# Three attentions with 16-bit value parts in column halves, odd units split by GpSimd, and norms from a sum of six squares

## The chip, the cores and the metric

The kernel runs on one core of one Trainium2 chip. The metric is device time in microseconds (us) of one execution, from the runs' own clock. A TensorE matmul has a stationary operand (loaded first) and a moving one that streams through; results go to PSUM, eight banks of 512 fp32 columns per partition. VectorE and ScalarE read PSUM; GpSimd works in SBUF alone.

## The reference, cut to what matters

512 tokens of width 1024 pass through two transformer blocks. The first has a sparse attention (8 heads of 64; each query attends to its 128 best keys of an index score, keys and values are shared by the heads), a pooling mixer and a layer of 16,384 small experts; the second has a windowed attention (16 heads on 4 key and value heads, window 128, a sink logit per head) and a latent attention (16 heads, query and key width 96, value width 64). Each block ends its parts with root-mean-square norms:

```python
p = jax.nn.softmax(logits, axis=-1)                       # all three attentions
o = jnp.einsum('...hqk,...khd->...qhd', p, v)             # 64 wide per head
h = h + (o * jax.nn.silu(z)) @ w_out                      # window and latent
y_attn = o @ w_up_attn                                    # sparse
y = x * lax.rsqrt(jnp.mean(x * x, axis=-1) + EPS) * g     # every norm, over 1024 features
```

## The kernel before, in words

Activations lie transposed: features on partitions (eight blocks of 128), 512 tokens in the free dimension. Dense products are made in 16-bit parts: each fp32 operand is split into a high part (the value rounded to 16 bit) and a low part (the rest), and `three` (line 830) issues three 16-bit matmuls, high x high, high x low, low x high. Weight tiles of 128 x 1024 come from memory into a ring of four (`ring`), GpSimd scales and splits them (`cut_tile`, lines 753 to 756) into a second ring of four (`parts`). A tile is cut when the tile three before it has begun to be used (`begun`).

`features_wide` starts a projection with the first five input blocks for four outputs, then finishes output by output; it takes a new weight tile per output, so it needs four tiles early. `tokens` makes rows by token: for a group of columns it first awaits four free banks and then sums into all four. Of each stage the sums are taken from PSUM by ScalarE or by VectorE, as a table at the top says (`taker`); a bank is free when that engine has taken its sum.

An attention is a list of units, one per head and block of 128 queries. For unit u in turn TensorE makes the scores in fp32 (`scores`, line 967, banks 4 and 5), VectorE takes the negated maximum (with mask or slope added in the sparse and window kinds; lines 1636, 1642, 1651), ScalarE the exponentials and their sum (line 1319), TensorE transposes the probabilities in blocks of 128 (`turn_probs`, line 976, banks 6 and 7), ScalarE copies them to SBUF (`copy`, line 1275), and TensorE multiplies them in fp32 with the values (`values`, line 988): the probabilities are stationary, 64 value columns move, and the output has tokens on partitions (bank 0 or 1, eight units to a bank). After eight units VectorE divides by the sums (lines 1668, 1671). The order on each engine is written out by hand: at step u TensorE does scores of u, transposes of u - 1 or u - 2 and values of the unit before that; the others follow by semaphores. In the latent kind each head's query and key rows are transposed first (lines 1237, 1240, banks 2 and 3) and copied by VectorE (line 2148), once per four units. GpSimd has no part in an attention.

When all units are done, the outputs are transposed back on TensorE (`turn`, line 959), VectorE multiplies them with the gate (line 2081, window and latent) and splits them (lines 1616, 1617), block by block, and the projection reads them.

Before the latent attention ScalarE takes queries, keys and values (`b_q`, `b_kv`) from PSUM, while VectorE rotates 32 columns of each query head (`rope`, lines 2124 to 2130).

A norm: ScalarE squares the eight blocks (line 1281), TensorE sums each over the partitions by a matmul with ones (`norm_part`, line 911, all eight summed in one bank), ScalarE takes the root, VectorE the reciprocal (line 1583), and then both make the split normed blocks that the next stage reads. The eight `norm_part` matmuls are placed between the outputs of the stage in front, two or more outputs behind the block that they square (`behind`, `late_pairs`, `last_parts`).

## Time and profile before

| | us |
|---|---|
| median of three runs | 2348.11 (2346.35 to 2356.07) |
| profiled execution, own time | 2350.81 |
| its span, first to last instruction | 2349.0 |
| TensorE busy | 2212.0 |
| VectorE busy | 1505.7 |
| GpSimd busy | 1372.1 |
| ScalarE busy | 909.2 |

The span is what the trace covers; the execution's own time also has what lies around it, 1.8 us. Matmuls are pipelined, so one lasts longer than the distance to the next. Read spacing by the starts. An fp32 matmul appears as two records. Of the span the sparse attention takes 222 to 275 us, the window attention 1704 to 1796, the latent one 2056 to 2212.

### The profile page before, as it was taken

To read this page: it belongs to the slowest core of one execution; us is meant where nothing else is said; L and a number is where in the kernel's file an instruction comes from. 1 tells how busy PE (TensorE), PEld (TensorE's weight loads), DVE (VectorE), ACT (ScalarE), POOL (GpSimd) and SP (SyncE) were. 2 spreads that over 40 slices of the span, in tenths; PEclk is the share of its full clock that TensorE was granted. 3 is DMA by queue.
4 is the path that set the end of the run, shared out by engine and by line. 5 is a ranking of instruction groups with operands and counts; after the bars stand their busy time and mean duration, and the time that the engine had idled before them with its cause. 6 is when DMAs were issued, how large, how long until landed. Compare 5 with 4: busy or idle time off the path is not lost. (4 is left out here: it accounts for less than half of the span.)

```text
span 2349.0 us, 36538 instructions
## 1 busy us (share of the span) xinstructions
PE 2212.0 (94%) x12904; PEld 1255.2 (53%) x12904; DVE 1505.7 (64%) x2703; ACT 909.2 (39%) x1582; POOL 1372.1 (58%) x872
## 2 busy tenths in 40 slices
PE   5998988999989999989999999998998989899897
PEld 2544634555556666545555555553576435477643
DVE  6597857999986776069899888832045344544523
ACT  2211412355556666533333333411174322355322
POOL 6885277678755555477778777635800758700072
PEclk9999999999999999999999999999999999999999
DMA  7333544589879999999999899822300323300021
GB/s 279 99 97 120 178 144 135 165 294 355 316 234 281 294 347 310 287 357 335 329 335 336 320 324 326 291 83 85 106 10 10 90 72 102 90 7 1 19 83 43
DMA packets 218054, 451.52 MB, mean 192 GB/s; under 512 B 83200, under 2 KB 132544, under 8 KB 217920
## 3 DMA queue, kind: packets, MB, share of 16 engines
q1 hardware_dynamic: 119696, 313.67, 39.1%
q0 software_dynamic: 27648, 100.68, 12.1%
q10 hardware_dynamic: 70576, 35.40, 6.2%
q8 instruction: 83, 1.36, 0.2%
q14 instruction: 51, 0.42, 0.1%
HBM read 390.86 MB, written 58.82 MB: 191 GB/s over the span
## 5 line engine op out<-in xcount | busy, mean ns | idle before, releaser
L830 PE MATMUL ps<-hT,parts 128*128 128x416 f16 (+1 forms) x4800 | 933.4, 355 | 29.1 <-POOL parts L756 10.2
L830 PEld LDWEIGHTS ps<-hT,parts 128*128 128x128 f16 x4800 | 467.3, 98 | 475.1 <-issue 24.6
L830 PE MATMUL ps<-arena 128*128 128x416 f16 x3072 | 545.8, 340 | 18.4 <-DVE arena L2031 14.0
L753 POOL TENSOR_SCALAR parts<-ring 128x1024 f16<-128x1024 f32 x141 | 160.9, 1141 | 591.3 <-PE ps L830 566.5
L830 PEld LDWEIGHTS ps<-arena 128*128 128x128 f16 x3072 | 300.7, 98 | 264.2 <-issue 20.0
L762 POOL TENSOR_TENSOR parts<-ring,parts 128x1024 f16<-128x1024 f32 x120 | 256.0, 2135 | 197.7 <-ACT ring L1432 197.2
L756 POOL TENSOR_TENSOR parts<-ring,parts 128x1024 f16<-128x1024 f32 x141 | 307.8, 2183 | 11.8
L788 POOL TENSOR_TENSOR arena<-ring,arena 128x1024 f16<-128x1024 f32 x128 | 295.5, 2319 | 25.2 <-ACT arena L1469 23.3
L2026 DVE TENSOR_TENSOR route<-arena 128x416 f32<-128x416 f32 x128 | 171.7, 1341 | 131.8 <-DMA arena<-gate_mem 126.7
L830 PE MATMUL ps<-arena,parts 128*128 128x512 f16 x876 | 198.9, 386 | 10.3 <-DVE arena L1806 4.6
L1484 ACT ACTIVATE arena<-route 128x416 f16<-128x416 f32 x128 | 70.3, 549 | 325.1 <-DVE route L2026 325.1
L1275 ACT ACTIVATE arena<-ps 128x512 f32<-128x512 f32 (+6 forms) x242 | 123.5, 524 | 172.3 <-PE ps L830 139.7
L2043 DVE SCALAR_TENSOR_TENSOR hT<-arena,spare,hT 128x1024 f32<-128x1024 f32 x93 | 187.6, 2017 | 0.0
L770 POOL DMA_INDIRECT arena<-v,spare x96 | 111.8, 1165 | 94.2 <-DVE hT L2043 78.2
L1411 ACT ACTIVATE spare<-ps 128x416 f32<-128x416 f32 x128 | 66.3, 518 | 250.7 <-PE ps L830 248.6
L754 POOL TENSOR_SCALAR ring<-ring 128x1024 f32<-128x1024 f32 x141 | 154.9, 1099 | 0.0
L830 PEld LDWEIGHTS ps<-arena,parts 128*128 128x128 f16 x876 | 86.3, 99 | 124.3 <-issue 19.3
L1469 ACT ACTIVATE arena<-ring 128x1024 f16<-128x1024 f32 x128 | 133.0, 1041 | 9.1 <-DMA ring<-v 9.1
L1431 ACT ACTIVATE parts<-ring 128x1024 f16<-128x1024 f32 x120 | 125.8, 1048 | 2.7 <-DVE xT L1965 2.7
L1642 DVE CUSTOM_DVE_ANT_0 arena<-ps,arena 128x256 f32<-128x256 f32 (+1 forms) x64 | 35.1, 550 | 141.7 <-PE ps L967 138.7
L2031 DVE TENSOR_TENSOR arena<-route,arena 128x416 f16<-128x416 f32 x128 | 121.5, 950 | 6.9 <-ACT arena L1484 6.9
L1432 ACT ACTIVATE ring<-ring 128x1024 f32<-128x1024 f32 x120 | 125.6, 1047 | 0.0
(208 smaller groups left out, 2598.7 us busy)
## 6 DMA issues: line engine op xcount, KB each, us to landing
ring<-w SPq DMA_DIRECT2D x133, 512.0 KB, 3.6
ring<-u SPq DMA_DIRECT2D x128, 512.0 KB, 6.4
ring<-v SPq DMA_DIRECT2D x128, 512.0 KB, 4.6
act_mem<-spare SPq DMA_DIRECT2D x128, 208.0 KB, 5.1
gate_mem<-arena ACTq DMA_DIRECT2D x4, 6656.0 KB, 50.8
arena<-act_mem SPq DMA_DIRECT2D x128, 208.0 KB, 4.2
arena<-gate_mem SPq DMA_DIRECT2D x128, 208.0 KB, 5.4
arena<-ada_w SPq DMA_DIRECT2D x48, 512.0 KB, 6.7
```

The lines of the kernel that those rows point to most:

```text
L753: G.tensor_scalar(dst[:, 0, :], src, WS, 1.0, ALU.mult, ALU.mult).then_inc(scaled, 1)
L754: G.tensor_scalar(src, src, WS, 1.0, ALU.mult, ALU.mult).then_inc(scaled, 1)
L756: G.tensor_tensor(dst[:, 1, :], src, dst[:, 0, :], ALU.subtract).then_inc(parts_ready, 1)
L762: G.tensor_tensor(dst[:, 1, :], src, dst[:, 0, :], ALU.subtract).then_inc(parts_ready, 1)
L788: G.tensor_tensor(dst[:, 1, :], src, dst[:, 0, :], ALU.subtract).then_inc(parts_ready, 1)
L830: ins = [T.matmul(out_, a, b, start=start and j == 0, stop=stop and j == 2) for j, (a, b) in enumerate(((lhs[0], rhs[0]), (lhs[0], rhs[1]) ...
L1275: return A.activation(dst, src, ACT.Copy, scale=scale)
L1431: A.activation(parts[:, n % RING, 0, :], src, ACT.Copy, scale=WS).then_inc(raised, 1)
L1432: A.activation(src, src, ACT.Copy, scale=WS).then_inc(raised, 1)
L1469: A.activation(v_parts[:, c % (2 * GROUP), 0, :], ring[:, (S_V + c) % RING, :], ACT.Copy).then_inc(v_high, 1)
L2026: V.tensor_tensor(prod[:, at % 2, :], pair[:, at % 4, 0, :], pair[:, at % 4, 1, :], ALU.mult).then_inc(product, 1)
L2043: V.scalar_tensor_tensor(out=sums, in0=row, scalar=w, in1=sums, op0=ALU.mult, op1=ALU.add).then_inc(rows_used, 1)
```

## The change

The values are split into 16-bit parts and become the stationary operand, 64 columns; the transposed probabilities are split too and move. Units are reordered: two heads by four query blocks form an eight, with the two heads of one block next to each other. For four units (two blocks, two heads) TensorE issues, per key block, three products for each head; the two heads' outputs go to partitions 0 to 63 and 64 to 127 of one bank, features on partitions. So the output is already transposed, and the transposes back go. The probabilities' transposes are now in banks 0 and 1, the outputs in 6 and 7.

Even units are split by ScalarE (high part, from PSUM) and VectorE (low part, from PSUM). Odd units are copied by ScalarE to a flat fp32 row, and GpSimd makes both parts from it. Between its units, once per attention, GpSimd cuts one weight tile.

The division moves behind the values: VectorE takes the reciprocals, TensorE spreads them over partitions by eight fp32 matmuls with the identity (bank 2, where the next heads' rows are also built), VectorE multiplies them with the gate in SBUF (ScalarE copies them in the sparse kind), then multiplies the output by that, ScalarE takes the high part and VectorE the low one. This is done once per eight, behind later units.

The window and latent values are taken by ScalarE (high) and VectorE (low, which then frees the bank); `b_kv` becomes `b_k` and `b_v`. In norms 1 to 6 VectorE adds squares 1 to 5 to square 0, and TensorE issues three matmuls with ones for the sum of six and the last two, behind the stage in front (or in the embedding product, for norms 3 and 5).

```diff
+            def attention(units, u0, between):                    # GpSimd
+                for u in range(1, len(units), 2):
+                    n = (u0 + u) // 2
+                    flat = in_blocks(flat_probsT(units[u], u))
+                    pool.wait_ge(probsT, u0 + u + 1)
+                    if u0 + u >= 2 * FOUR:
+                        pool.wait_ge(attended, (u0 + u) // FOUR - 1)
+                    G.tensor_scalar(probsT_out(units, u, 0), flat, 1.0, 1.0, ALU.mult, ALU.mult).then_inc(flat_high, 1)
+                    pool.wait_ge(flat_high, n + 1)
+                    G.tensor_tensor(probsT_out(units, u, 1), flat, probsT_out(units, u, 0),
+                                    ALU.subtract).then_inc(flat_cut, 1)
+                    if u == 9:
+                        between()
...
-                    if u0 + u >= 2:
+                    if u0 + u >= 2 and u % 2:                     # turn_probs
                         pe.wait_ge(probsT, u0 + u - 1)
+                    elif u0 + u >= 2:
+                        pe.wait_ge(probs_low, (u0 + u) // 2)
...
+                def values(u, second):
+                    blocks = blocks_of_four(units, u)
+                    base = first_block(units, u)
+                    at = units[u]["i"] * P
+                    if not second:
+                        pe.wait_ge(probs_low, (u0 + u + FOUR) // 2)
+                        pe.wait_ge(flat_cut, (u0 + u + FOUR) // 2)
+                        if u % EIGHT == 0 and u0 + u >= 2 * EIGHT:
+                            pe.wait_ge(o_ready, (u0 + u) // EIGHT - 1)
+                    for n in (range(2, len(blocks)) if second else range(min(2, len(blocks)))):
+                        c, i0, i1 = blocks[n]
+                        for t, (v_part, p_part) in enumerate(((0, 0), (0, 1), (1, 0))):
+                            for s in range(2):
+                                mm = T.matmul(o_bank(u // EIGHT)[s * 64:s * 64 + 64, at + i0 * P:at + i1 * P],
+                                              value_rows(units[u + s], c, v_part),
+                                              probsT_of(units[u + s], u, p_part)[:, c - base, i0 * P:i1 * P],
+                                              start=(n == t == 0), stop=(n == len(blocks) - 1 and t == 2))
+                    if second == (len(blocks) > 2):
+                        mm.then_inc(attended, 1)
+
+                def spread_rates(u):
+                    b = (u0 + u) // EIGHT
+                    pe.wait_ge(recips, b + 1)
+                    if b > 0:
+                        pe.wait_ge(rates_used, b)
+                    if units[u]["kind"] == "latent":
+                        pe.wait_ge(turned_read, turns[0])
+                    by = eight_totals(units[u], u)
+                    for i in range(NT):
+                        for s in range(2):
+                            mm = T.matmul(rates_bank[s * 64:s * 64 + 64, i * P:(i + 1) * P],
+                                          by[:, 2 * i + s:2 * i + s + 1].broadcast_to([P, 64]), ident[:, :],
+                                          start=True, stop=True)
+                    mm.then_inc(rates_spread, 1)
...
+                    if 2 <= u < len(units) + 2:
+                        turn_probs(u - 2)
+                    if u >= EIGHT and u % EIGHT == 1:
+                        spread_rates(u - 9)
+                    if u >= 7 and u % FOUR == 3:
+                        values(u - 7, False)
+                    if u >= 8 and u % FOUR == 0:
+                        values(u - 8, True)
...
+                if h >= 4:                                        # head_rows
+                    pe.wait_ge(rates_used, O_LATENT + h // 2 - 1)
...
+            for s in range(2 * NT):                               # VectorE, behind the rope of q
+                dve.wait_ge(v_high_rows, NT + s + 1)
+                b = take("b_v", s)
+                cols = slice((s // NT) * 512, (s // NT + 1) * 512)
+                own.do(V.scalar_tensor_tensor(out=vlat[:, s % NT, 1, cols], in0=b, scalar=1.0 / WS,
+                                              in1=vlat[:, s % NT, 0, cols], op0=ALU.mult, op1=ALU.subtract), took["dve"])
...
+                def low_probs(u):                                 # VectorE
+                    un = units[u]
+                    dve.wait_ge(probsT, u0 + u + 1)
+                    own.do(V.tensor_tensor(probsT_out(units, u, 1), in_blocks(ps[:, u % 2, 0:un["nc"] * P]),
+                                           probsT_out(units, u, 0), ALU.subtract), probs_low)
...
+                for u in range(len(units) + 8):                   # VectorE, after maxima(u)
+                    if 3 <= u < len(units) + 3 and u % 2:
+                        low_probs(u - 3)
+                    if 1 <= u <= len(units):
+                        normalise(u - 1)
                     if hook is not None:
                         hook(u)
+                    b, at = u // EIGHT - 1, u % EIGHT
+                    if b >= 0 and at == 3:
+                        rate(b)
+                    if b >= 0 and at == 5:
+                        gate(b)
+                    if b >= 0 and at == 7:
+                        low(b)
...
+            def add_square(n, k):                                 # VectorE
+                if 1 <= k < ADDED:
+                    dve.wait_ge(squares, KC * n + k + 1)
+                    own.settle()
+                    first = squares_of(n)[:, 0, :]
+                    own.do(V.tensor_tensor(first, first, squares_of(n)[:, k, :], ALU.add),
+                           squares_added if k == ADDED - 1 else None)
...
+            def all_parts(n):                                     # TensorE
+                added_part(n)
+                for k in range(ADDED, KC):
                     norm_part(n, k)
...
-            pe.wait_ge(o_ready, O_END)
-            t_o = turns[0]
-            for b in range(KC):
-                turn([(i, btok[:, i, b * P:(b + 1) * P]) for i in range(NT)])
-            features_wide("b_out", in_parts(bz), lambda k: pe.wait_ge(turned_read, t_o + k + 1), late_pairs(5))
+            pe.wait_ge(rates_used, O_END)
+            features_wide("b_out", in_parts(bz), lambda k: pe.wait_ge(o_ready, O_LATENT + k + 1))
+            features("ple_w1", in_parts(pT), lambda k: pe.wait_ge(p_ready, 2 + k + 1), parts_behind(5))
+            features_wide("ple_g1", hr, h_need(5))
+            all_parts(6)
```

## Rows read from the trace of the kernel before

**Rows 1.** The page's first part: busy us, share of the span, instructions.
```profile
PE 2212.0 (94%) x12904; PEld 1255.2 (53%) x12904; DVE 1505.7 (64%) x2703; ACT 909.2 (39%) x1582; POOL 1372.1 (58%) x872
```
**Rows 2.** Busy time by stretch: us, PE, PEld, DVE, ACT, POOL, clock, DMA, GB/s.
```profile
222.00:275.00 53.00, 49.53 (x322) 39.66 (x321) 39.16 (x108) 31.66 (x96) 0.00 (x0) 0.97 0.70 231
...
1708.00:1796.00 88.00, 87.14 (x606) 73.86 (x606) 43.85 (x157) 62.93 (x195) 0.00 (x0) 1.00 0.01 1
...
2057.00:2212.00 155.00, 153.06 (x1019) 118.92 (x1018) 68.62 (x110) 81.14 (x192) 0.00 (x0) 1.00 0.00 1
...
2212.00:2227.00 15.00, 8.74 (x41) 4.77 (x40) 14.16 (x22) 0.00 (x0) 4.18 (x3) 0.77 0.12 35
```
**Rows 3.** TensorE in order of time, latent attention: start, us, line, operation.
```profile
2124.42 1.08 PE L967 MATMUL ps<-arena,spare 96*128 96x512 f32 x2
2125.33 0.60 PE L976 MATMUL ps<-ident,arena 128*128 128x128 f32 x4
2125.77 1.00 PE L988 MATMUL ps<-hT,arena 128*128 128x64 f32 x8
2126.61 0.60 PE L1237 MATMUL ps<-ident,arena 128*96 128x128 f32 x4
...
2127.48 1.02 PE L967 MATMUL ps<-arena,spare 96*128 96x512 f32 x2
```
**Rows 4.** The chain that ended last, in order of time: start, us, what.
```profile
1599.30 50.03 PE ps L830 x231
```
**Rows 5.** TensorE and its weight loads in order of time, around 477 us.
```profile
477.44 1.09 PE L1131 MATMUL ps<-xT,hT 128*32 128x128 f16 x64
...
477.44 0.91 PEld L1131 LDWEIGHTS ps<-xT,hT 128*32 128x32 f16 x64 [0.34 <-issue]
```
**Rows 6.** VectorE in order of time, in the sparse and the latent attention.
```profile
249.32 1.28 DVE L1693 CUSTOM_DVE_ANT_0 arena<-arena,route,vecs 128x1024 f32<-128x1024 f32 x1
...
2129.15 0.68 DVE L2148 COPY spare<-ps 96x512 f32<-96x512 f32 x1
2129.75 0.68 DVE L2148 COPY arena<-ps 96x512 f32<-96x512 f32 x1
```
**Rows 7.** TensorE and GpSimd in order of time, behind the window and latent attention.
```profile
1792.93 1.20 PE L988 MATMUL ps<-arena 128*128 128x64 f32 x8
...
1811.49 4.69 PE L830 MATMUL ps<-arena,parts 128*128 128x512 f16 x21 [1.55 <-POOL parts L756]
...
2208.72 1.99 PE L988 MATMUL ps<-hT,arena 128*128 128x64 f32 x16
...
2221.64 4.05 PE L830 MATMUL ps<-arena,parts 128*128 128x512 f16 x9
2226.88 3.40 PE L830 MATMUL ps<-arena,parts 128*128 128x512 f16 x15 [1.19 <-POOL parts L756]
...
2222.47 1.05 POOL L753 TENSOR_SCALAR parts<-ring 128x1024 f16<-128x1024 f32 x1 [169.15 <-PE ps L830]
...
2224.61 2.12 POOL L756 TENSOR_TENSOR parts<-ring,parts 128x1024 f16<-128x1024 f32 x1
```
**Rows 8.** VectorE and TensorE in order of time, ahead of the latent attention.
```profile
2027.21 0.42 DVE L2124 TENSOR_TENSOR arena<-arena 128x256 f32<-128x256 f32 x1 [19.51 <-ACT arena L1275]
...
2028.73 2.35 DVE L2126 TENSOR_TENSOR arena<-arena 128x256 f32<-128x256 f32 x1
...
2050.20 1.14 DVE L2130 TENSOR_TENSOR arena<-arena 128x256 f32<-128x256 f32 x1
...
2048.20 5.34 PE L830 MATMUL ps<-parts,arena 128*128 128x512 f16 x24 [0.89 <-ACT hT L1275]
```
**Rows 9.** TensorE in order of time, norms 3 and 4.
```profile
1854.42 1.88 PE L911 MATMUL ps<-hT,ones 128*128 128x512 f32 x4
...
1868.22 2.12 PE L830 MATMUL ps<-hT,parts 128*128 128x512 f16 x9
...
1910.93 1.88 PE L911 MATMUL ps<-arena,ones 128*128 128x512 f32 x4
```

More of the change, by code:

```diff
@@ new lines, in in_blocks, with first_block, probsT_out, blocks_of_four @@
+        def in_blocks(row):
+            return row.rearrange("p (c q) -> p c q", q=P)
+        def first_block(units, u):
+            return min(units[u]["c0"], units[u + 2]["c0"])
+        def probsT_out(units, u, part):
+            un = units[u]
+            c = un["c0"] - first_block(units, u - u % FOUR)
+            i = un["i"] % 2
+            return probsT_of(un, u, part)[:, c:c + un["nc"], i * P:(i + 1) * P]
+        def blocks_of_four(units, u):
+            a, b = units[u], units[u + 2]
+            blocks = lambda un: range(un["c0"], un["c0"] + un["nc"])
+            both = [(c, 0, 2) for c in blocks(a) if c in blocks(b)]
+            return both + [(c, 0, 1) for c in blocks(a) if c not in blocks(b)] + [(c, 1, 2) for c in blocks(b)
+                                                                                  if c not in blocks(a)]
@@ L992, in attention @@
-                late = lag(units)
-                for u in range(len(units) + late + 1):
+                def values(u, second):
[17 more added lines that the diff above has]
+                        mm.then_inc(attended, 1)
@@ L994, in attention @@
+                for u in range(len(units) + 5):
                     if hook is not None:
@@ L1338, in attention @@
                         exps_of(u)
-                    if late == 1 and u >= 1:
-                        copy_probs(u - 1)
+                    b, at = u // EIGHT - 1, u % EIGHT
+                    if b >= 0 and at == 2 and units[0]["kind"] == "sparse":
+                        act.wait_ge(rates_spread, u0 // EIGHT + b + 1)
+                        own.do(copy(scr[:, b % 2, :], rates_bank, scale=1.0), rates_used)
+                    if b >= 0 and at == 6:
+                        act.wait_ge(o_gated, u0 // EIGHT + b + 1)
+                        own.do(copy(halves(parts_of[:, b, :])[0], o_bank(b), scale=1.0), o_high)
             act.wait_ge(x_loaded, 16)
@@ L1675, in attention, with rate @@
-                late = lag(units)
-                for u in range(len(units) + late + 1):
+                    own.do(V.reciprocal(tot, tot), recips)
+                def low_probs(u):
+                    un = units[u]
+                    dve.wait_ge(probsT, u0 + u + 1)
+                    own.do(V.tensor_tensor(probsT_out(units, u, 1), in_blocks(ps[:, u % 2, 0:un["nc"] * P]),
+                                           probsT_out(units, u, 0), ALU.subtract), probs_low)
+                def rate(b):
+                    if gates_of is not None:
+                        dve.wait_ge(took["act"], count_taken(gates_of, b))
+                        dve.wait_ge(rates_spread, u0 // EIGHT + b + 1)
+                        own.do(V.tensor_tensor(parts_of[:, b, :], rates_bank, parts_of[:, b, :], ALU.mult), rates_used)
@@ L1823, in cut_turned @@
                 cut_block(dst, ps[:, 4 + (r_ - 1) % 4, :], signal=turned_read)
-            for b in range(4):
-                cut_turned(halves(oT[:, b, :]))
             for m in range(KC):
```

313 lines of the change are left out of this document (162 added, 151 removed).

## The prediction

> **What bounds the kernel now.** The busy shares come first: TensorE 94%, VectorE 64%, GpSimd 58%, ScalarE 39% [rows 1]. These are averages, so the busy time per stretch comes next. In the window attention TensorE is busy for 87.14 of 88 us, in the latent attention for 153.06 of 155, at full clock, with GpSimd idle; between the latter and its output projection stand 15 us in which TensorE is busy for 8.74 and VectorE for 14.16, at a mean clock of 0.77 [rows 2]. So inside these two attentions a TensorE microsecond is a microsecond of the run; behind them VectorE sets the pace. The sparse attention has VectorE at 39 of 53 us beside a TensorE at 49.5. TensorE's order in time then prices one latent unit: 0.91 us of scores, 0.44 of transposes, 0.84 of values, 2.19 in all, and 0.87 for the rows of each head [rows 3]. Eight units with two heads' rows take 8 x 2.19 + 2 x 0.87 = 19.3 us; eight times that is 154, the stretch in rows 2. A window unit is 88 / 64 = 1.375 us.
>
> **Values in halves.** Per unit and key block the old kernel issues two 64-column fp32 records (8 records in 0.84 us, 0.105 each). The new one issues, per four units and key block, three 16-bit products for each of two heads: 24 matmuls of 256 moving columns in the latent attention. A 512-column 16-bit matmul takes 50.03 / 231 = 0.217 us [rows 4], so 256 columns take 0.108 if the two column halves run one behind the other. The trace has one place with columns in parts: 64 matmuls of 128 columns, each into a quarter of the array, in 1.09 us [rows 5]. One behind the other they would take 64 x 0.054 = 3.5 us; they ran over three times as fast. Two halves should therefore run side by side. Bounds for four latent units: 24 x 0.108 / 2 = 1.3 us and 24 x 0.108 = 2.6. I take 1.3 plus 0.3 for the two changes between full and half array (1.09 - 0.86 = 0.23 for the pair of changes in that row), 1.6 us against 3.36 before.
>
> The Trainium skill (TensorEngine Tiling (Array Packing), Key Properties) says that changing the tiling mode drains the engine while tiles of one mode work in parallel. By it the price would be the same 1.3 us and a drain per change that it does not size; the row bears out the parallel part and leaves at most 0.23 us for two drains.
>
> New is the spreading of softmax rates: eight fp32 matmuls of 128 columns per eight units. No row has this form; the nearest is the pair of 0.105 us records, 0.21 each, 1.7 us one behind the other and 0.85 side by side. I take 0.9.
>
> Latent, per eight units: scores 7.3, transposes 3.5, head rows 1.74, values 3.2, rates 0.9 and 0.2 for their change: 16.8 against 19.3, 2.5 x 8 = **-20 us**. Window: scores average 320 of 512 columns, 0.57 us, transposes 2.5 x 0.11 = 0.28; 18 value matmuls per four (12 of 256, 6 of 128 columns) are 0.8 + 0.3 us; per eight 4.6 + 2.2 + 2.2 + 1.1 = 10.1, I take 10.5 for the short ones, against 11.0: **-4 us**.
>
> **What this sets against it.** VectorE gets, per eight latent units, four subtractions for even units, a rate, a gate and a low part, seven more passes over 512 columns at 0.6 us pitch (two copies start 0.60 apart [rows 6]), minus the old normalisation: 8 x 0.6 + 4 x 0.6 + 4 x 0.6 + 3 x 0.6 + 0.2 = 11.6 us of 16.8. It fits, but five consecutive steps hold 1.8 us each. One place is a wait: the rates use bank 2, in which the next heads' rows are built, so TensorE must wait at step 4 for VectorE's rate of step 3, which stands behind a maximum and a subtraction: some 0.9 us, 8 times, 7 us. ScalarE is busy 81.14 / 64 = 1.27 us per unit [rows 2] and gets one more copy per eight, 10.8 of 16.8: hidden. GpSimd splits an odd unit in one pass and one subtraction; it has 1.05 and 2.12 us for 1024 columns [rows 7], so half, 1.6 us, and 0.2 for its waits, per 4.2 us (latent) or 2.6 us (window). Bounds: 1.6, and 3.2 if the width does not matter. I take 1.8, since both groups scale by width elsewhere; it is idle there now. Behind the ninth unit a weight tile of 4.3 us is inserted on its queue; odd units 11 and 13 wait for it and the values for them: 1.5 us each attention. Other unevenness 1.5 us each. Stalls: **+10** latent, **+3** window.
>
> **Starts.** The low parts of the latent values are eight VectorE passes queued behind the rotation of q. That ends only at 2051.3 us, since its two-input SBUF operations stretch from 0.42 to 2.35 us when GpSimd is busy [rows 8]. TensorE's last value group, begun at 2048.20 [rows 8], needs four banks that VectorE now frees: four passes after about 2050 (GpSimd's last tile there is moved into the attention), so 2052.6: +4.4. The last low part adds 0.75, and two heads' rows are built before the first unit, of which each waits for two copies: +2.1. Sum **+7.2**. The window's value rows add **+0.5**.
>
> **Tails.** The old kernel ends the latent values at 2210.7, then transposes, gates and cuts eight blocks; the projection has its ninth matmul early and the rest from 2226.88, when GpSimd has cut the fourth weight tile [rows 7]. In the new one seven of eight blocks are ready before the last values end, and the projection starts with five of them for four outputs. GpSimd's tile is still asked for only when the projection begins: 2226.88 - 2221.64 = 5.24 us from its start to the resumption. So 16.2 - 5.35 = 10.8 us go; the next thing that is late is that tile. Off this: the last odd unit passes GpSimd (1.7 us) and its four units' values follow: 2.1 more from the last scores to the values' end. **-8.7**. In the window the same count is 1811.49 - 1794.1 = 17.4 [rows 7], minus 5.35, minus 1.2 (256 columns): **-10.8**.
>
> **Sparse.** VectorE there gets 16 subtractions (about 0.42, 6.8 us) and eight passes for gate and low part (5.0) and loses four (2.5): 48.5 of 53 us, so it becomes the bound, and the modulation's two-input operations (1.28 us [rows 6]) now meet GpSimd. The body grows by about 3, the four transposes with their cuts (5 us) go, the drain grows by 1.5: **-1**.
>
> **Norms.** Eight fp32 matmuls become three; a pair of them costs 1.72 us (1.88 with the end that the next overlaps [rows 9]) and the one behind the last square ends the chain. For norms 1 and 2 five leave the inside of the loop (4.3) and the tail, with the sum of six ready when the last square is, grows from little over one to three: +1.6. So -2.7 each. Norms 4 and 6: 3.44 go, the tail takes three instead of one, less waiting for the table load: -2.1 each. Norms 3 and 5 lie before a short projection: 3.44 go from the loop, and the segment from 1854.4 to 1868.2 [rows 9] becomes bound by the reciprocal chain instead of TensorE, 13.3 against 13.8: -4 each. Together -17.6. VectorE's additions read two SBUF rows: 0.69 us as other passes of 512 columns, more beside GpSimd, where 256 columns took 2.35 [rows 8]. Only the last addition of a norm is on the path; I add 0.7 for norms 3 and 5: **-16.2**.
>
> The rule that speaks against these additions is in the Trainium skill (SBUF — State Buffer, SBUF: two separate sides): VectorE with two SBUF inputs and GpSimd exclude each other for a whole instruction. Rows 8 agree, 0.42 against 2.35 us. If each of the six last additions met a 2.1 us subtraction, the norms would give -6 instead of -16; that stays inside the range.
>
> **Sum.** Latent -20 + 10 + 7.2 - 8.7 = -11.5; window -4 + 3 + 0.5 - 10.8 = -11.3; sparse -1; norms -16.2: -40.0. The profiled execution is 2350.81 us (span 2349.0 and 1.8 around it), 2.7 above the median of 2348.11. 2350.81 - 40.0 = 2310.8; two thirds of the offset off, **2309 us**.
>
> **Rivals.**
> Halves one behind the other: values +2.6 and rates +0.8 per eight latent units (+27), 1.6 and 0.8 in the window (+19), less the 7 us of waiting for the rate, which then hides: -40 + 39, **2348 us**. For it: no row has 64-column halves with different moving rows. Against: the 64 matmuls in 1.09 us.
> GpSimd becomes the bound: at 3.2 + 0.4 us per odd unit its 32 units of the window take 115 us against 85 forecast (+30), 16 sparse ones 58 (+6); the latent stays hidden: **2345 us**. For it: each output has a strided four-block pattern in 16 bit, absent from the trace. Against: 1.05 us per 1024 columns.
> Slower: the weights of a half are not loaded while the other half computes. Then each value matmul pays its load of 0.1 us as well (24 loads and matmuls at 0.2 = 4.9 us per four latent units, 18 at 0.19 = 3.4 in the window), +52 and +37 against forecast: **2398 us**. It decides from 40 / 672 = 0.06 us above the 0.055 per matmul, that is at 0.115 us each. Against it: in rows 5 the 64 loads fit into 0.91 of the same 1.09 us.
> That the maths is not what it says (the weight path stays in fp32) is excluded by the types in the diff.
>
> **Chances.** Forecast 0.78, halves in series 0.09, GpSimd 0.07, slower 0.06. The forecast's own range is 2284 (no stalls, no delayed start: -25) to 2332 (values at the middle of their bounds, or all last additions blocked and the stalls doubled). To leave out no more than 2 in 10 the range goes to 2340. A change under 0.5% (11.7 us) cannot be told from none. Faster by more: 2309's case nearly whole and part of the GpSimd case, 0.82; within: 0.11; slower: 0.07.
>
> **What would show it.** After the change: value matmuls (the new one at their line) at 24 in about 1.5 us per four latent units; eight latent units at 18 us; the projection starting within 1 us of the last values and one wait for GpSimd's tile behind it; a wait of TensorE for VectorE's rate before the head rows; last value group of the latent stage starting 4 us late; three ones-matmuls per norm. A value matmul at 0.108 us spacing, a GpSimd split over 2.6 us, or a sparse attention over 58 us would make the prediction wrong.

## The result, and the profile after

The changed kernel takes 2329.24 us in the median of 9 runs, the kernel before in the same session 2349.85: ratio 0.9914, 95% interval 0.9894 to 0.9935. That is 20.6 us less where 40 were forecast (2309); the time lies inside the stated range of 2284 to 2340 and the direction was right, the size was not: half of the gain is missing. The profiled execution took 2325.09 us, span 2323.1.

Page of the changed kernel, first part, against [rows 1]: TensorE is busy 51 us less, VectorE 71 and GpSimd 126 more.

```profile
PE 2160.9 (93%) x12908; PEld 1182.5 (51%) x12908; DVE 1576.3 (68%) x2807; ACT 920.3 (40%) x1606; POOL 1497.8 (64%) x1032
```

Busy time by stretch of the changed kernel, columns as in [rows 2]: sparse attention, window attention and its tail, latent attention and its tail.

```profile
220.00:278.00 58.00, 46.75 (x354) 30.65 (x355) 48.15 (x125) 35.77 (x103) 28.33 (x35) 0.94 0.63 211
1698.00:1797.00 99.00, 89.20 (x705) 59.48 (x706) 68.36 (x207) 67.96 (x208) 44.03 (x67) 0.98 0.02 7
1797.00:1811.00 14.00, 11.08 (x51) 4.88 (x52) 5.71 (x6) 0.60 (x1) 4.22 (x3) 1.00 0.13 39
2052.00:2199.00 147.00, 138.84 (x996) 88.23 (x998) 93.63 (x155) 84.17 (x199) 60.89 (x67) 0.97 0.02 5
2199.00:2212.00 13.00, 10.13 (x60) 4.75 (x56) 3.96 (x6) 0.60 (x1) 4.17 (x3) 1.00 0.25 82
```

Before, TensorE was busy for 99% of both attentions. Now it is for 94% of the latent one, which got shorter (150.4 to 139.5 us from first to last score), and for 90% of the window one, which got longer (87.8 to 93.7). Cut at the same instructions in both traces, the run changed like this (us; a norm ends at its reciprocal, and norm 2 begins at VectorE's first sum behind the experts):

| stretch | forecast | measured |
|---|---|---|
| sparse: first score to VectorE's first pass of the next projection | -1 | +2.2 |
| norms 1 / 2 | -2.7 / -2.7 | +0.5 / -3.0 |
| norms 3 and 5, each | -3.3 | -3.7 |
| norms 4 and 6, each | -2.1 | -0.2 |
| window: start, first to last score, tail | +0.5, -1, -10.8 | +0.3, +5.9, -9.8 |
| latent: start, first to last score, tail | +7.2, -10, -8.7 | +9.85, -10.85, -7.65 |
| sum | -40.0 | -20.3 |

The rest of the span's -25.9 (-5.6) lies outside the change: from norm 1's reciprocal to norm 2's, nearly all of it the experts' part, the profiles below took 1230 to 1242 us. (The first products in front of norm 2 took 5.57 us at a mean clock of 0.73 in the kernel before and 4.22 at 1.00 in the changed one; that is not counted as the norm's gain.) So stretches are compared from here on, and times with their intervals.

A stretch comes from one profiled execution of each version. The steady groups of eight units repeat within about 0.01 us, but stretches that hold a wait of TensorE can differ by 1 to 3 us with the granted clock behind it, without an edit there: norm 2 took 38.65 us in the changed kernel and 40.2 to 40.4 in three versions below that leave it alone; the latent attention's first score rows ran at clock 0.50 in the changed kernel and at 1.00 in others, which is worth 2.65 us. Differences below of that size in such a place are not shown to be an edit's.

TensorE of the changed kernel in order of time, steady window units (columns as in [rows 3]; in brackets the idle time before and who ended it), and VectorE in front of the wait:

```profile
1748.24 1.09 PE L1090 MATMUL ps<-ident,arena 128*64 128x128 f32 x16 [0.21 <-DVE arena L1774]
1749.26 0.91 PE L1045 MATMUL ps<-arena 128*128 128x384 f32 x2
...
1750.23 0.81 PE L1045 MATMUL ps<-arena 128*128 128x384 f32 x2
...
1751.19 0.85 PE L1073 MATMUL ps<-arena 128*64 128x256 f16 x12
1751.96 0.91 PE L1045 MATMUL ps<-arena 128*128 128x384 f32 x2
...
1753.13 0.36 PE L1073 MATMUL ps<-arena 128*64 128x128 f16 x6
...
1754.50 0.60 PE L1045 MATMUL ps<-arena 128*128 128x256 f32 x2
1755.62 0.52 PE L1056 MATMUL ps<-ident,arena 128*128 128x128 f32 x3 [0.52 <-DVE arena L1779]
...
1759.93 1.09 PE L1090 MATMUL ps<-ident,arena 128*64 128x128 f32 x16 [0.21 <-DVE arena L1774]
...
1754.37 0.62 DVE L1752 CUSTOM_DVE_ANT_0 arena<-ps,arena 128x384 f32<-128x384 f32 x1 [0.83 <-PE ps L1045]
1754.91 0.55 DVE L1779 TENSOR_TENSOR arena<-ps,arena 128x384 f16<-128x384 f32 x1
```

Twelve products of 256 columns take 0.77 us from first to next line, 0.064 each. From one spreading of rates (L1090) to the next are 11.69 us: 10.96 of work and 0.73 idle. Before, eight window units took 88 / 64 x 8 = 11.0. The work has not shrunk: from the start of a group to the next, values fell from 4.06 to 2.13 us, but the rates are new (1.02), and scores and transposes cost 5.00 and 2.81 instead of about 4.7 and 2.2, because half-array products stand next to them (another 0.16 of the scores is the end of the rows in front of the wait, which nothing overlaps). It does not take the 16-bit type: the rates are half-array products in fp32 as their neighbours are, and a pair of score rows takes 0.91 us behind them (1749.26) as behind values (1751.96), against 0.81 behind transposes (1750.23). The idle time sits behind VectorE's low part (L1779), queued behind the maximum of unit 5 (L1752).

Around the weight tile that GpSimd cuts behind odd unit 9, same kernel, GpSimd and TensorE:

```profile
1714.73 1.04 POOL L808 TENSOR_SCALAR parts<-ring 128x1024 f16<-128x1024 f32 x1
...
1718.97 0.52 POOL L852 TENSOR_SCALAR arena<-arena 128x384 f16<-128x384 f32 x1
1719.57 0.91 POOL L854 TENSOR_TENSOR arena<-arena 128x384 f16<-128x384 f32 x1
...
1718.08 0.49 PE L1056 MATMUL ps<-ident,arena 128*128 128x128 f32 x3
1720.58 0.85 PE L1073 MATMUL ps<-arena 128*64 128x256 f16 x12 [2.01 <-issue]
...
1722.89 1.22 PE L1045 MATMUL ps<-arena 128*128 128x256 f32 x2
```

Odd unit 11 waits from 1714.7 to 1719.0. TensorE idles 2.01 us (the profile says "issue"; what is late is GpSimd's subtraction, 0.91 from 1719.57), and then the pair of score rows behind the next group of values takes 1.22 us instead of 0.70. The granted clock, in the same kernel's row for that stretch, is 0.50, its lower level:

```profile
1722.00:1725.00 3.00, 3.00 (x19) 1.88 (x19) 1.60 (x7) 1.29 (x5) 0.00 (x0) 0.50 0.08 30
```

### The profile page after: what moved, and what is told of

The parts are those of the page before. It is cut to its first block and busy times, and to the rows that moved or that the text cites. A ratio compares the mean times of both kernels' runs of the same rounds, so it can differ in the third digit from the quotient of the medians.

```text
span 2323.1 us, 36974 instructions
## 1 busy us (share of the span) xinstructions
PE 2160.9 (93%) x12908; PEld 1182.5 (51%) x12908; DVE 1576.3 (68%) x2807; ACT 920.3 (40%) x1606; POOL 1497.8 (64%) x1032
## 5 line engine op out<-in xcount | busy, mean ns | idle before, releaser
L1375 ACT ACTIVATE arena<-ps 128x512 f32<-128x512 f32 (+9 forms) x266 | 135.9, 532 | 246.8 <-PE ps L908 141.7
L908 PE MATMUL ps<-arena,parts 128*128 128x512 f16 x876 | 193.5, 381 | 11.6 <-POOL parts L811 5.8
L2186 DVE SCALAR_TENSOR_TENSOR hT<-arena,spare,hT 128x1024 f32<-128x1024 f32 x93 | 193.9, 2085 | 0.0
L852 POOL TENSOR_SCALAR arena<-arena 128x512 f16<-128x512 f32 (+3 forms) x80 | 43.9, 549 | 191.0 <-ACT arena L1375 191.0
L809 POOL TENSOR_SCALAR ring<-ring 128x1024 f32<-128x1024 f32 x141 | 161.3, 1144 | 0.0
L2013 DVE CUSTOM_DVE_ANT_0 arena<-arena,ps 128x1024 f32<-128x1024 f32 x96 | 115.9, 1216 | 14.7 <-DMA arena<-u_rows,spare 8.4
```

The costliest lines, as they stand in the source:

```text
L809: G.tensor_scalar(src, src, WS, 1.0, ALU.mult, ALU.mult).then_inc(scaled, 1)
L908: ins = [T.matmul(out_, a, b, start=start and j == 0, stop=stop and j == 2) for j, (a, b) in enumerate(((lhs[0], rhs[0]), (lhs[0], rhs[1]) ...
L1375: return A.activation(dst, src, ACT.Copy, scale=scale)
L2186: V.scalar_tensor_tensor(out=sums, in0=row, scalar=w, in1=sums, op0=ALU.mult, op1=ALU.add).then_inc(rows_used, 1)
```

## The experiments

In all but the first the base is the changed kernel. The two theories behind them: the missing 20 us are order (who stands behind whom in VectorE's and GpSimd's queues, and the clock that TensorE loses behind each wait), or they are work in the new shape of the products. By the whole time alone only the column halves apart, the two tiles and the three combined versions differ from the changed kernel (0.9894 to 0.9935); the other intervals overlap that, and what is said of them rests on stretches.

**Norms alone on the kernel before.** Its norms were replaced by the new ones (six squares added, three ones-matmuls), the attentions left.

> The kernel before with the change's norms alone: VectorE adds the first six squares, TensorE takes three ones-matmuls a norm; the attentions are as before. If the forecast sized the norms rightly (-16.2 us) and the attentions gave it back, the ratio is 0.993. If the two traces tell the truth (norm 1 +0.5, norm 2 -3.0, norm 3 -3.7, norm 4 -0.2, norms 5 and 6 -3.9), it is -10 us, ratio 0.9957, and norm 1 and norm 4 show TensorE idle 3 us and more behind VectorE's last addition and then ones-matmuls of about 0.9 to 1.2 us instead of 0.43.

2340.42 us, ratio 0.9949 (0.9930 to 0.9969). By stretch: norm 1 +2.0, norm 2 -3.0, norms 3 and 5 -3.7 each, norm 4 -0.2, norm 6 +2.3: -6.3 us. So the traces' reading holds, in stretches less than half of the -16.2 forecast; norms 1 and 6 came out 1.5 and 2.5 us longer than in the changed kernel. The ratio's interval, -7 to -16 us, does not decide by itself.

**VectorE: low part first.**

```diff
                 for u in range(len(units) + 8):
+                    if 3 <= u < len(units) + 3 and u % 2:
+                        low_probs(u - 3)
                     if u < len(units):
                         maxima(u)
-                    if 3 <= u < len(units) + 3 and u % 2:
-                        low_probs(u - 3)
```

> The changed kernel with VectorE's low part of an even unit (u-3) ahead of the maximum of unit u instead of behind it, in all three attentions. Theory A (TensorE's turn waits for a low part that stands behind a maximum in VectorE's queue): in the window attention the time from one eight's rates to the next falls from 11.7 us to 10.9 to 11.2, the stretch from first to last score from 93.7 to 88 to 90 us, the sparse attention by up to 1 us. Rival B (TensorE's own work in column halves sets 11.7 us): within 1 us of 93.7.

2327.29 us, 0.9906 (0.9881 to 0.9930), no difference from the changed kernel's 0.9914. Eight window units went from 11.69 to 11.40 us, the window's body from 93.7 to 91.2 (A's direction, less than its size), the latent body by -1.5, the sparse one by -0.7. Of the 0.73 us idle 0.23 went; the rest moved from the transposes to the values. The tails gave 1.8 and 1.4 back: in the window's, TensorE waits the same 2.92 us for the weight tile, but with a granted clock of 0.50 behind it (1.00 in the changed kernel).

**GpSimd's tile ahead of the attentions.**

```diff
-                cut_tiles(done, first, CHUNKS, CHUNKS - RAISED)
-                attention(units, u0, lambda: cut_tiles(first, first + 1, CHUNKS, CHUNKS - RAISED))
+                cut_tiles(done, first + 1, CHUNKS, CHUNKS - RAISED)
+                attention(units, u0, lambda: None)
```

> The changed kernel with GpSimd's one weight tile cut just ahead of each attention instead of behind the odd unit 9. Theory A (the tile holds the odd units of the second and third four up): the first two eights of the window attention take 2 to 3 us less (14.6 and 12.0 us before the steady 11.7), the sparse attention up to 1.5 us less, the latent attention 0 to 1 less, nothing is lost at the starts. Rival B (GpSimd is idle enough for the tile, the first eights are long for another reason, filling): no stretch changes by over 0.5 us, or the start of the window attention is 1 to 4 us later since the tile now delays odd unit 1.

2323.61 us, 0.9898 (0.9871 to 0.9925). Window body 93.67 to 90.42 us (first eight 11.69 like the steady ones), sparse body 47.48 to 44.47, latent body +0.2, latent start +1.0 (as in the version with five squares, which has no edit there), window start unchanged. Theory A: the tile cost 3.25 us in the window's body and 3.0 in the sparse one, and nothing in the latent one. In the sparse attention part comes back behind the body: up to VectorE's first pass of the next projection it is 1.5 us less here, as expected, and 2.8 with two tiles ahead, whose sparse part is the same.

**Latent value low parts between the rotary rows.**

```diff
+            q_rope(0)
+            q_rope(1)
             for s in range(2 * NT):
+                if s == NT:
+                    q_rope(2)
+                    q_rope(3)
```

> The changed kernel with VectorE's four low parts of the first latent value group put between the second and the third rotary row, not behind the fourth. Theory A (the second value group waits for banks that VectorE empties behind the rotary rows): its start is 3.5 to 4 us earlier after the first group, TensorE's 5.28 us wait is 1.4 to 1.8, and since it idles less the group runs in about 5.4 us instead of 6.88; norm 4's reciprocal to the first latent score is 4 to 5.5 us shorter than 143.0. Rival B (the group waits for ScalarE's 16-bit parts or for GpSimd's weight parts, or the rotary rows moved behind the group are late for the head rows): under 1 us shorter, or longer.

2324.86 us, 0.9890 (0.9863 to 0.9916). First the changed kernel around its last value group, TensorE and VectorE, which answer to [rows 8]:

```profile
2039.61 6.88 PE L908 MATMUL ps<-parts,arena 128*128 128x512 f16 x24 [5.28 <-DVE hT L2289]
...
2052.66 5.74 PE L1045 MATMUL ps<-arena,spare 96*128 96x512 f32 x6 [0.78 <-DVE arena L2296]
...
2032.27 2.23 DVE L2271 TENSOR_TENSOR arena<-arena 128x256 f32<-128x256 f32 x1
...
2036.87 2.48 DVE L2289 SCALAR_TENSOR_TENSOR hT<-ps,hT 128x512 f16<-128x512 f32 x4
```

Then the same with the order changed:

```profile
2042.94 5.34 PE L908 MATMUL ps<-parts,arena 128*128 128x512 f16 x24 [1.61 <-DVE hT L2294]
...
2054.09 1.98 PE L1045 MATMUL ps<-arena,spare 96*128 96x512 f32 x4 [0.94 <-DVE arena L2301]
...
2040.05 2.63 DVE L2294 SCALAR_TENSOR_TENSOR hT<-ps,hT 128x512 f16<-128x512 f32 x4 [4.37 <-PE ps L908]
2042.78 0.43 DVE L2265 TENSOR_TENSOR arena<-arena 128x256 f32<-128x256 f32 x1
```

The wait fell from 5.28 to 1.61, the group from 6.88 to 5.34, norm 4's reciprocal to first score from 142.97 to 137.37 us: theory A with its numbers. The first scores ran at the upper clock this time (1.98 us for four rows; before 5.74 for six) and the latent body got 2.6 us shorter too; the tail got 1.5 longer. That 2.6 is not shown to be this edit's: the version that keeps TensorE busy in norms 1, 4 and 6, further down, still has the long wait (5.24 us), and its first scores run the same way:

```profile
2053.25 1.99 PE L1048 MATMUL ps<-arena,spare 96*128 96x512 f32 x4 [0.94 <-DVE arena L2299]
```

**Five squares added instead of six** (`ADDED = 5`).

> The changed kernel with VectorE adding five squares of a norm instead of six, so that TensorE takes four ones-matmuls. Theory A (VectorE's addition of the sixth square ends 2 to 3.6 us after TensorE's last projection product; TensorE idles, its granted clock falls and all six rows of ones run at 0.86 us instead of 0.43): with five the sum is ready before the last square, TensorE has work at once and waits for the last square alone; norm 1's last-ones-to-reciprocal chain is 3 to 4 us shorter, norm 4's 4 to 5 us, norm 6's 3 to 4, norm 2's 0 to 1.5, norms 3 and 5 at most 0.9 longer: -10 to -14 us. Rival B (one ones-matmul more costs what the earlier sum saves, the path is the last square and the square root's table): -2 to +3 us.

2320.42 us, 0.9880 (0.9860 to 0.9899). Norm 1 -4.0, norm 2 -0.8, norm 4 -3.2, norm 6 -1.6, norms 3 and 5 +1.5 and +1.6: -6.5 us, theory A with half to two thirds of its size (norms 4 and 6 gave less than it said, norms 3 and 5 lost 1.6 instead of at most 0.9). Norm 4 of the changed kernel, VectorE's last addition and TensorE:

```profile
1901.98 1.41 DVE L1974 TENSOR_TENSOR arena<-arena 128x512 f32<-128x512 f32 x1
...
1903.44 2.08 PE L1001 MATMUL ps<-arena,ones 128*128 128x512 f32 x2 [3.64 <-DVE arena L1974]
1905.31 3.62 PE L989 MATMUL ps<-arena,ones 128*128 128x512 f32 x4
```

and with five squares:

```profile
1897.06 1.02 PE L1001 MATMUL ps<-arena,ones 128*128 128x512 f32 x2
1897.91 1.88 PE L989 MATMUL ps<-arena,ones 128*128 128x512 f32 x4
1900.46 1.13 PE L989 MATMUL ps<-arena,ones 128*128 128x512 f32 x2 [0.66 <-ACT arena L1381]
```

Eight rows of ones now end earlier behind the projection than six did: the sum is there before TensorE runs dry, so both the wait and the lower clock go.

**TensorE kept busy in front of the ones** (12 products of 128 columns that nobody uses).

```diff
             def added_part(n):
+                if n in (1, 4, 6):
+                    for _ in range(12):
+                        T.matmul(norm_bank(n)[:, 0:P], ones[:, :], ident[:, :], start=True, stop=True)
                 pe.wait_ge(squares_added, n)
```

> The changed kernel in which TensorE, in norms 1, 4 and 6, makes 12 products of 128 columns that nobody uses (2.6 us) while it waits for VectorE's last addition. Theory A (the six rows of ones run at the half clock because TensorE idled 2.9 to 3.6 us just before): their start stays as it was, but they run at 0.43 us each, and norms 1, 4 and 6 are 2 to 2.6 us shorter each, some -6 us. Rival B (the half clock is set by the busy stretch before, or has another cause): rows of ones still at 0.86, no gain.

2324.32 us, 0.9895 (0.9878 to 0.9912). Granted clock of norm 4's ones in the changed kernel (columns as above):

```profile
1903.00:1909.00 6.00, 5.49 (x6) 1.85 (x6) 0.39 (x1) 0.03 (x1) 2.37 (x1) 0.50 0.43 141
```

and with the idle time filled, the clock and TensorE in order of time:

```profile
1904.00:1911.00 7.00, 6.03 (x33) 3.94 (x31) 2.81 (x3) 3.12 (x5) 6.04 (x4) 1.00 0.25 80
```

```profile
1904.38 2.84 PE L1002 MATMUL ps<-ident,ones 128*128 128x128 f32 x24
1908.20 1.13 PE L1004 MATMUL ps<-arena,ones 128*128 128x512 f32 x2 [0.97 <-DVE arena L1977]
1909.16 1.88 PE L989 MATMUL ps<-arena,ones 128*128 128x512 f32 x4
```

The six rows ran 0.43 us apart in all three norms, where norm 4's had been 0.85 apart and those of norms 1 and 6 had started so: start of ones to reciprocal 6.25 to 3.60 us in norm 4, 5.28 to 3.60 in norm 6. Idling is the cause of the half clock there. It did not pay in full: norm 1 kept a gain of 1.4 us, norm 4 half of its own, norm 6 nothing, and the projections ahead of norms 4 and 6 now lost clock behind an older 3 us wait that had cost none in the changed kernel (1.00 at 1859 to 1863 us there; here ahead of norm 4):

```profile
1863.00:1866.00 3.00, 2.44 (x6) 0.87 (x7) 2.93 (x6) 1.19 (x2) 0.41 (x1) 0.50 0.48 122
```

**Column halves apart** (each head's products in a row instead of the two heads by turns).

```diff
-                    for n in (range(2, len(blocks)) if second else range(min(2, len(blocks)))):
-                        c, i0, i1 = blocks[n]
-                        for t, (v_part, p_part) in enumerate(((0, 0), (0, 1), (1, 0))):
-                            for s in range(2):
+                    for s in range(2):
+                        for n in (range(2, len(blocks)) if second else range(min(2, len(blocks)))):
+                            c, i0, i1 = blocks[n]
+                            for t, (v_part, p_part) in enumerate(((0, 0), (0, 1), (1, 0))):
```

> The changed kernel with the values' loops turned round: all products of one head (one column half), then all of the other, instead of the two halves by turns. Theory A (two column halves run side by side only where neighbours in TensorE's queue use different halves): 12 products of 256 columns take 1.3 us instead of 0.78, eight latent units 18.1 + 2.1 = 20.2 us, eight window units 11.7 + 1.6 = 13.3, the time 30 to 40 us longer. Rival B (0.065 us a product is the rate of issue, or a half is as fast alone): the same within 3 us.

2342.63 us, 0.9975 (0.9964 to 0.9986): 13 us longer than the changed kernel, between the two theories. TensorE in its latent attention:

```profile
2096.93 1.09 PE L1073 MATMUL ps<-arena,hT 128*64 128x256 f16 x12
2097.95 1.13 PE L1045 MATMUL ps<-arena,spare 96*128 96x512 f32 x2
```

In the changed kernel the two heads' products start 0.003 us apart and the next pair 0.106 later; apart, behind the first product's 0.13, they start after 0.11, 0.006, 0.10, 0.03, 0.08, 0.03, 0.08 us and so on. Values per eight latent units rise from 3.17 to 4.15 us, not to 5.2; eight latent units take 18.82 us instead of 18.08, eight window units 11.94 instead of 11.69. Of the 13 us the latent body has 2.75 (its first scores ran at the upper clock here, which saves 2.65), the window's 0.4 and the two tails 2.2 and 1.9; the rest lies outside the attentions. So neighbours in different halves do run side by side. Starts 0.006 us apart where the queue holds six products of one half suggest that TensorE starts some of the later half's products early by itself; the trace does not say which half a product uses.

**Two tiles ahead.** As in the third experiment, and in window and latent attention the projection's fourth tile as well, behind the sums of the projection before (`cut_tile(last, last + CHUNKS, 0, CHUNKS - RAISED, stages[name].s0)`, which waits for those sums instead of the next tile's first product).

> The changed kernel with GpSimd's weight tile behind odd unit 9 cut ahead of each attention, as before, and in the window and latent attentions also the projection's fourth tile ahead (its slot is free when the last sum of the projection before is done). Theory A (the one wait left in those tails is GpSimd's fourth tile, 2.92 us in the window): TensorE starts the projection and does not stop for a tile; window tail 2.5 to 3.5 us shorter than with the first tile alone ahead, latent tail likewise 2 to 3.5. Rival B (the projection then waits for the gate and low part of the last block instead, or odd unit 1 of the window is held by the second tile): under 1 us in the tails, or the window's first eight longer by up to 2 us.

2313.70 us, 0.9853 (0.9833 to 0.9874). TensorE in the window's tail of the changed kernel, which answers to [rows 7]:

```profile
1796.94 2.12 PE L908 MATMUL ps<-arena,parts 128*128 128x512 f16 x9
1801.98 10.30 PE L908 MATMUL ps<-arena,parts 128*128 128x512 f16 x47 [2.92 <-POOL parts L811]
```

and with two tiles ahead:

```profile
1790.95 15.28 PE L911 MATMUL ps<-arena,parts 128*128 128x512 f16 x70
```

No stop: both tails are 3.0 us shorter, the window body 3.3, the sparse one 2.9. Theory A.

**The four together.**

> The changed kernel with five squares added, both tiles ahead, the latent low parts between the rotary rows and the low part of an even unit ahead of the maximum. If the mis-sized steps are order and not work, their gains add: norms -12, window body -3.3 and tail -3, sparse -3, latent start -5.6 and tail -2.5, low parts first -0.5: about -28 us against the changed kernel, near 2300 us, ratio to the kernel before 0.980. If they hide one another, under half of that.

2307.34 us, 0.9822 (0.9805 to 0.9840): -22 us against the changed kernel, not -28. One gain is missing. TensorE, VectorE and GpSimd ahead of the latent attention:

```profile
2041.54 1.06 PE L1342 MATMUL ps<-ident,arena 128*96 128x128 f32 x4 [8.69 <-DVE hT L2297]
...
2035.46 2.33 DVE L2270 TENSOR_TENSOR arena<-arena 128x256 f32<-128x256 f32 x1
...
2035.35 2.17 POOL L813 TENSOR_TENSOR parts<-ring,parts 128x1024 f16<-128x1024 f32 x1
```

The tile moved ahead meets the rotary rows that were moved behind: VectorE's operation of 0.42 us takes 2.33 beside GpSimd's subtraction, TensorE idles 8.69 us, and the start of the latent attention is 146.2 us instead of 137.4.

**The same, mended.**

> e8 with two mends: in the latent attention both weight tiles stand behind odd unit 9 again (in e8 GpSimd cut the fourth beside the rotary rows, and the latent start was 146.2 us instead of e4's 137.4), and norms 3 and 5 add six squares again, the others five. Theory A (VectorE's rotary rows and GpSimd's tile hold each other up, and TensorE then idles 8.7 us): latent start 137 to 138.5 us, latent body 136 to 139, latent tail as in e7, norms 3 and 5 each 1.5 us shorter than in e8; about 2296 us, ratio 0.977 to 0.980. Rival B (the latent start was lost to the low parts put early): start stays over 143, about 2304 us.

2297.85 us, 0.9790 (0.9774 to 0.9805). Start 138.0 us: theory A. But two tiles in a row inside the latent attention stretch the eight units around them to 24.4 us, against 17.85 for the others, and its body misses its 136 to 139 us with 142.0; one tile had cost nothing.

**Values in one place.** All products of four units at one step, on the changed kernel and on the mended one.

```diff
                         values(u - 7, False)
-                    if u >= 8 and u % FOUR == 0:
-                        values(u - 8, True)
+                        values(u - 7, True)
```

> The changed kernel with all value products of four units in one place, instead of two blocks at one step and the rest at the next. Theory A (each change between whole-array and half-array products costs TensorE about 0.1 us, at the end of the transposes before and at the head of the scores behind): one pair of changes less for each four units, steady eight window units 11.7 - 0.4 = 11.3 us, eight latent units 18.1 - 0.4 = 17.7: -3 us in each, -1 to -2 in the sparse attention. Rival B (no price of a change; the scores behind a group are long since they wait for VectorE): the same times, or longer, as the burst of 1.6 us makes VectorE and ScalarE wait for scores.

2321.88 us, 0.9891 (0.9873 to 0.9908). TensorE in its window attention:

```profile
1751.63 1.01 PE L1073 MATMUL ps<-arena 128*64 128x256 f16 x18
1752.57 0.70 PE L1045 MATMUL ps<-arena 128*128 128x256 f32 x2
...
1753.32 0.60 PE L1045 MATMUL ps<-arena 128*128 128x256 f32 x2
```

TensorE's work per eight window units fell from 10.96 to 10.33 us: with two groups of half-array products less, transposes lost 0.19, scores 0.20 and values 0.24, so 0.31 us a group. (The score rows behind the group take 0.70, those behind transposes 0.60.) Idle time rose from 0.73 to 1.05, so eight window units take 11.37 us, as theory A said. Eight latent ones take 17.24 instead of 18.08, twice its gain: 0.41 less work, and 0.43 less idle time of TensorE. The bodies are 3.8 and 8.4 us shorter; 2.65 of the 8.4 are the first scores, at the upper clock in this execution and not shown to be the edit's.

> e9 with the value products of e10. By theory A of e10 -5 to -8 us against e9; by its rival 0 or longer.

**2292.62 us**, 0.9768 (0.9751 to 0.9786): the fastest version, 37 us under the changed kernel and 57 under the one before. It is 5 us under the mended one, theory A's lower end; the two intervals just overlap, but the eights agree with it, 11.19 and 17.0 us instead of 11.40 and 17.85. Its page, and TensorE behind the two tiles in the latent attention:

```profile
PE 2144.9 (94%) x12916; PEld 1180.8 (52%) x12916; DVE 1572.4 (69%) x2803; ACT 921.4 (40%) x1606; POOL 1492.0 (65%) x1032
```

```profile
2054.04 0.60 PE L1068 MATMUL ps<-ident,arena 128*128 128x128 f32 x4
2058.63 2.77 PE L1085 MATMUL ps<-arena,hT 128*64 128x256 f16 x24 [3.99 <-issue]
```

That wait of 3.99 us, with the values behind it at half the clock (2.77 us; 1.50 for the group before), is what it still leaves; tiles further apart were not tried.

## Why the prediction was off

Its picture was right in the main. The rows of [rows 5] were a good witness that column halves run side by side: 24 products in 1.58 us (1.6 forecast, though that had the neighbours' share of the changes in it), eight latent units in 18.08 (18), 0.86 of waiting for the rate (0.9), GpSimd 0.62 + 1.16 us a latent odd unit (1.8), both projections starting right behind the last values with one wait for GpSimd's tile. Latent body, both tails and norms 3 and 5 came within 1.1 us of their terms. None of the rivals happened. For the latent body part of that is luck: work per eight was 17.2 us where 16.8 were forecast (transposes 4.0 instead of 3.5), 3.4 us in all, and the first scores lost 2.65 at the lower clock; against that, the 3 us set aside there for the tile and unevenness were hardly needed (the tile moved away changed it by +0.2), and more of the last units' values falls behind the last score.

The step that failed is the pair of terms for the window attention's body, "**-4 us**" of work and "Stalls: ... **+3** window". It was to be -1 and became +5.9 us.
- Work, -4: none of it came (10.96 us per eight units against 11.0). I had taken 10.1 and gone to 10.5 "for the short ones", with the change between full and half array in it once per four units, at 0.3 us. That price was right, the count was not: the code has two groups of value products per four units, and the rates, and a group costs 0.31 us, most of it in the scores and transposes next to it, whose prices I had left as they were (4.6 + 2.2 us forecast, 5.0 + 2.8 measured). Values and rates themselves came out as forecast. The Trainium skill (TensorEngine Tiling (Array Packing), Key Properties) says that changing the tiling mode drains the engine. The trace agrees, and the experiment with values in one place gives the size here, the 0.31 us.
- Stalls, +3: the inserted tile alone was 3.25, of it part idling and part the lower clock behind, where I had 1.5; and 0.73 us per eight, some 5.8 in all, came from low parts and reciprocal in VectorE's queue, where I had 1.5 for all other unevenness. Turning the order round took 0.23 of the 0.73 away; what is left was not taken apart. I had checked that VectorE's sum fits, not in which order its passes stand.

The body also hands work to the tail (the last units' values), so these do not add up to +5.9 exactly.

Second, the norms, -16.2 forecast and -10.3 measured in the changed kernel. "The tail takes three instead of one" left out that TensorE runs dry: TensorE waits 2.9 to 3.6 us for VectorE's last addition in norms 1, 4 and 6, and behind that wait the three ones-matmuls run at the lower clock, all or in part, 0.85 us a row instead of 0.43. So these norms gained nothing, though five matmuls had gone. Keeping TensorE busy showed the clock's part (2.65 us in norm 4's ones); adding one square less removes the wait and the clock's loss together. The addition is longer beside GpSimd (1.41 us in norm 4, 0.93 for the one before it), as the 0.7 us allowed, but only for norms 3 and 5.

Third, smaller: the sparse attention (+2.2 for -1), where the tile was in no term (3.0 us of the body, 1.5 to 2.8 of the stretch), and the latent start (+9.85 for +7.2), where the wait for VectorE's low parts was foreseen and the half clock of the value group (6.88 us instead of 5.34) and of the second head's rows behind it was not.

Of the 19.7 us missing in the stretches, 6.9 are thus the window's body, 5.9 the norms, 3.2 the sparse attention, 2.65 the latent start; 1.0 is spread over the rest.

## What to carry to other kernels

When matmuls shrink to a part of the array, count how often the queue changes between shapes, and gather the small ones: here a change to halves and back cost as much as five of the products. When TensorE gets faster, what bounds is the order in the other engines' queues: put what TensorE waits for ahead of what only keeps the engine busy, and foreign work (a weight tile) where nobody waits. Price a new wait twice, once for the idling and once for what may run behind it at the lower clock, and look for two mended orders that meet each other.

## What the runs showed of the hardware that was not expected

- Two products for different column halves start 0.003 us apart and share 0.106 us; in an unfavourable order part of them still overlap (twelve in 1.02 us, 0.78 in the good order).
- In the window attention a group of half-array products among full-array ones costs 0.31 us beyond its own products, split between the transposes before, itself and the scores behind.
- The granted clock fell to 1.2 GHz behind waits of TensorE of about 2 us (window, 1720) as well as 3 to 9 us, but not behind all of them: the 2.92 us in the window's tail cost no clock in the changed kernel and did with VectorE's new order (0.50 from 1800 to 1803 us), and norm 2's wait of 1.53 us, the same in both, left the six rows behind it at 2.81 us in the changed kernel and let them take 4.5 in the version with TensorE kept busy, which has no edit there. What decides between them stayed open.
